# Moving the weight buffers of a two-stack transformer kernel by 64 bytes

## The reference, cut to what matters

```python
def first_block(x, ...):
    for layer in range(DEPTH):                  # 2 layers
        h = rms_norm(x, attn_norm[layer])
        if layer % 2 == 0:
            z = h @ w_in_e[i]                   # 1024 x 2072
            ...
            x = x + mix @ w_out_e[i]
        else:
            z = h @ w_qkv_o[j]                  # 1024 x 3072
            ...
            x = x + c_out.astype(x.dtype) @ w_out_o[j]
        h = rms_norm(x, ffn_norm[layer])
        gate, up = jnp.split(h @ w_gate_up[layer], 2, axis=-1)   # 1024 x 5632
        x = x + (jax.nn.silu(gate) * up) @ w_down[layer]         # 2816 x 1024
    return rms_norm(x, final_norm)

def compress_blocks(t, pe, w1, w2):
    ...
    return jax.nn.silu(blocks @ w1) @ w2        # w1: 2048 x 256
```

## Time and profile before

| what | value |
|---|---|
| median of 3 runs | 2921.04 us (2920.51 to 2929.26) |
| the profiled execution, device time | 2932.0 us |
| its span, first to last instruction | 2930.2 us |
| TensorE, matmuls | 2762.4 us busy (94%), 13516 matmuls |
| TensorE, weight loads | 2252.8 us busy (77%) |
| VectorE, ScalarE, GpSimd | 37%, 37%, 46% busy |
| mean granted TensorE clock | 0.967 |

### The profile page before, as it was taken

How to read it: one execution, slowest core, us unless ns; L and a number is a source line. 1 busy time by engine, 2 the same in 40 slices (tenths; PEclk the granted TensorE clock), 3 DMA queues, 4 the chain that set the end, 5 groups by cost and what they waited for, 6 DMA issues and landing times.

```text
span 2930.2 us, 37914 instructions
## 1 busy us (share of the span) xinstructions
PE 2762.4 (94%) x13516; PEld 2252.8 (77%) x13516; DVE 1078.1 (37%) x1941; ACT 1085.9 (37%) x1766; POOL 1345.6 (46%) x715
## 2 busy tenths in 40 slices
PE   7999999999999999999998999999978689999998
PEld 5756888888757888878767888888866588788886
DVE  5674322113563222023447234221074573432212
ACT  5665332223663322232243333332226343332221
POOL 4555444444384444444445544444433364344442
PEclk9999999999999999999889999999999799999998
DMA  4301323333202233323213312223312231223331
GB/s 156 122 2 39 97 95 100 100 108 97 86 1 83 93 100 100 101 79 102 71 37 101 108 58 86 92 95 105 104 51 79 80 125 62 65 94 100 100 101 64
DMA packets 69089, 251.77 MB, mean 86 GB/s; under 512 B 7672, under 2 KB 7928, under 8 KB 68736
## 3 DMA queue, kind: packets, MB, share of 16 engines
q1 hardware_dynamic: 67104, 244.35, 25.9%
q10 hardware_dynamic: 1888, 6.14, 0.6%
HBM read 248.36 MB, written 2.10 MB: 85 GB/s over the span
## 4 chain that ended last, share of the span: by engine, by line
PE 86%; DVE 9%; issue 2%; ACT 2%; POOL 1%; DMA 0%; DVEq 0%; POOLq 0%; ACTq 0%
PE ps L548 26%; PE ps L550 25%; PE ps L549 25%; PE ps L686 4%; PE ps L711 2%; PE ps L697 2%; DVE acc L1373 1%; DVE xl L1380 1%; POOL pr L514 1%; DVE u_r L1839 1%; DVE u_r L1837 1%; DVE tmpb L1862 0%; DVE pr L1473 0%; DVE y_mid L1683 0%; PE ps L656 0%
## 5 line engine op out<-in xcount | busy, mean ns | idle before, releaser
L467 POOL TENSOR_TENSOR w_lo<-w_raw,w_hi 128x1024 fp32r<-128x1024 f32 x462 | 1115.2, 2418 | 1382.5 <-ACT w_hi L980 1367.4
L548 PE MATMUL ps<-xh,w_hi 128*128 128x512 f32 x2384 | 940.0, 394 | 50.4 <-DVE xl L1380 21.6
L549 PE MATMUL ps<-xl,w_hi 128*128 128x512 f32 x2384 | 933.3, 391 | 0.0
L550 PE MATMUL ps<-xh,w_lo 128*128 128x512 f32 x2384 | 933.0, 391 | 0.0
L980 ACT ACTIVATE w_hi<-w_raw 128x1024 fp32r<-128x1024 f32 x462 | 484.5, 1053 | 531.0 <-PE ps L550 530.3
L548 PEld LDWEIGHTS ps<-xh,w_hi 128*128 128x128 f32 x2384 | 451.5, 189 | 150.3 <-issue 52.5
L549 PEld LDWEIGHTS ps<-xl,w_hi 128*128 128x128 f32 x2384 | 451.5, 189 | 94.3 <-issue 1.7
L550 PEld LDWEIGHTS ps<-xh,w_lo 128*128 128x128 f32 x2384 | 450.8, 189 | 94.9
L548 PE MATMUL ps<-hh,w_hi 128*128 128x512 f32 x704 | 273.9, 389 | 0.0
L550 PE MATMUL ps<-hh,w_lo 128*128 128x512 f32 x704 | 273.9, 389 | 0.0
L549 PE MATMUL ps<-hl,w_hi 128*128 128x512 f32 x704 | 273.9, 389 | 0.0
(11 more groups left out here) (258 smaller groups left out, 2910.4 us busy)
## 6 DMA issues: line engine op xcount, KB each, us to landing
w_raw<-weights_in SPq DMA_DIRECT2D x462, 512.0 KB, 3.4
x<-x_in ACTq DMA_DIRECT2D x4, 512.0 KB, 10.4
mem<-mem_in ACTq DMA_DIRECT2D x2, 1024.0 KB, 4.9
x_out<-x SPq DMA_DIRECT2D x4, 512.0 KB, 2.6
rope<-rope_in ACTq DMA_DIRECT2D x1, 512.0 KB, 11.8
tab<-tables_in ACTq DMA_DIRECT2D x2, 256.0 KB, 2.9
tab<-tables_in ACTq DMA_DIRECT2D x1, 384.0 KB, 12.4
small<-small_in ACTq DMA_DIRECT2D x1, 326.5 KB, 5.1
```

The source lines that it names most:

```text
L467: nc.gpsimd.tensor_tensor(w_lo[:, slot], w_raw[:, slot], w_hi.bitcast(f32)[:, slot], ALU.subtract).then_inc(lo_ready, 1)
L548: nc.tensor.matmul(dst, w_hi[:, slot, w], hi, start=first, stop=False)
L549: nc.tensor.matmul(dst, w_hi[:, slot, w], lo, start=False, stop=False)
L550: return nc.tensor.matmul(dst, w_lo[:, slot, w], hi, start=False, stop=last)
```

## The change

Two small buffers of 64 bytes per partition are allocated, one ahead of the three ring buffers and one behind them. Nothing reads or writes them. `w_raw`, `w_hi` and `w_lo` move up by 64 bytes and so begin on odd multiples of 64; everything allocated behind them moves up by 128 bytes and `x` stays. No instruction is added, removed or reordered, and no shape changes.

```diff
         x = sb("x", [P, KT, T])
+
+        sb("off_line", [P, 16])
         w_raw = sb("w_raw", [P, RING, CW])
         w_hi = sb("w_hi", [P, RING, CW], f32r)
         w_lo = sb("w_lo", [P, RING, CW], f32r)
+        sb("on_line", [P, 16])
         xl = sb("xl", [P, KT, T], f32r)
         rope = sb("rope", [P, 2, T])
         rstd = sb("rstd", [P, T])
```

## The result

The change makes the kernel slower: median 2941.2 us (2937.3 to 2943.5, 6 runs) against 2925.5 us (2920.5 to 2929.3, 6 runs, the three of the forecast and three more) before, a ratio of 1.0053, 95% interval 1.0038 to 1.0068. That is 15.7 us. The forecast was no change, 2921 us.

What follows compares the result with a forecast made beforehand. TensorE's matmuls, busy 2762.4 of 2930.2 us, were taken to bound the kernel. Every term was taken at 0, so the forecast stood on the median, 2921 us, with a range of 2905 to 2958.

Steps and rivals of the forecast that it cites:

- What bounds the kernel: TensorE's matmuls, busy 2762.4 of 2930.2 us; only their spacing, or a transfer or engine becoming late, could matter.
- Transfers: Weight chunks land 3.4 us after issue, with more than 10 us between issue and need; cost 0.
- ScalarE: `high` on the weight chunks takes 1.05 us and was expected not to depend on the address; cost 0.
- GpSimd: `low` on the weight chunks, cover thin only in the memory projections; taken at 0, at most 26 us.
- the price of a load by itself: Weight loads on TensorE beginning off a 128-byte line; price taken 0.
- Everything behind the weights: Buffers allocated after the weights move by 128 bytes, from an odd to an even multiple of 128; cost 0.
- the moving operands: They stay on multiples of 128 except 96 matmuls in `compress`; taken at 0, at most 9.6 us.
- The surcharge: 13.3 ns beyond the columns for each 512-column `product` matmul, 132 us over 9,936; change taken as 0.
- The argument from proportion: Time beyond the columns at full clock grows with stationary columns: 13.3 ns for 128, half for 64, whatever the moving columns.
- the block rival: Each weight load touches five 128-byte blocks instead of four, 3.3 ns each: 36 us slower, 2957 us; chance 0.11.
- The faster rival: Weight load and moving stream no longer collide in reading: up to 132 us less, 2789 us; chance 0.13.
- The 31-column loads: Half begin 124 bytes past a multiple of 128, yet all take 105 to 109 ns: no price for an off-line load.

Runs made afterwards that it cites:

- both off: Weights and every moving operand moved by 64 bytes (only the buffer ahead of the weights kept), against the kernel before: ratio 1.0001 (0.9992 to 1.0011).
- the first experiments: Three kernels against before, 64 bytes off: weights and moving operands 1.0001, only the moving operands 1.0053, only the raw chunks 1.0004.
- bare stream: Not the kernel: the reference's work left out, dense matmuls in the pattern of `product` with operand places varied; 226.7 ns at distance 0, 512 float32r columns.

## Why the prediction was wrong, point by point

**What bounds the kernel: right.** The time followed the spacing of the `product` matmuls, beside the granted clock of the attention stages, which varies from one execution to the next.

**Transfers, ScalarE, GpSimd, the price of a load by itself: right at 0.** The raw chunks alone off gave 1.0004, and both off 1.0001.

**Everything behind the weights, and the moving operands: not nothing.** The forecast took 128 bytes for a neutral step, since the moving operands stay on multiples of 128. The distance counts within 256 bytes: moving only what lies behind the weights by 128 costs 5.7 ns a matmul. In the change the weights move by 64 and the moving operands by 128, which makes the distance -64 and costs 2.2 ns; moving operands that had stayed modulo 256 would have made it 64, which costs 6.7. It is the second small buffer, placed to put them back on multiples of 128, that makes the distance: with the first alone both move by 64, and nothing is paid. In `compress`, where 64 stationary columns meet slices of the weights, the steps within a chunk went from 114.0 to 118.3 ns on average; that is 0.4 us for its 96 matmuls.

**The surcharge: named as the one place where the change could act, and priced wrongly.** The step that failed is the sentence that "whichever half the load begins in, the two meet for the same share of the time". It averages over two steady streams, and the spacing is not steady: it follows a repeating pattern, 226.7 each time at distance 0 and 226, 229, 232 in the change, and which pattern it is changes with the distance of the two starts. Whether the two wait for each other in it was not shown. The term was taken at 0 and measures 2.22 ns for each 512-column matmul: 9,936 x 2.22 = 22 us by the forecast's own count.

Of these 22 us the median shows 15.7 and the two profiled runs 11.3 (2943.3 - 2932.0). The traces tell where the rest went. Both have the same 13,516 matmuls in the same order and can be compared step by step. The 9,745 steps between 512-column matmuls of `product` that are at full clock in both are 21.3 us longer in sum, nearly the whole term. The steps outside `product` are 6.7 us shorter in sum, the rest of `product` about 3 us. A matmul at half clock pays nothing. And the attention stages, whose operands did not move against one another, ran at a better clock; here is one window after (row above: 69.7 us at 0.76 before), 1.2 us of it:

```profile
1447.00:1515.50 68.50, 63.14 (x385) 40.77 (x384) 29.41 (x106) 31.27 (x92) 35.29 (x32) 0.78 0.03 9
```

The same stage took 61.0 us at 0.89 in the profiled run with both off, so that it varies without any change of spacing. The clock also hides a part of the term in the medians: the runs of the change have a mean clock of 0.971 to 0.974, the 23 of before that ran beside the first experiments 0.965 to 0.971. At the same mean clock the term is whole. At 0.971 two runs of before took 2922.7 and 2924.0 us and one of the change 2943.5; at 0.970 six of before took 2924.4 to 2925.4 and three with the moving operands off, which have the distance of the change, 2947.0 to 2948.6. Why the kernels at distance -64 were granted the better clock stays open.

**The argument from proportion** (13.3 ns for 128 stationary columns, half for 64) held only where it was read. The bare stream has it again with 256 moving columns at distance 0 (120.0 and 113.3 ns), but at distance 64 the order is reversed (113.3 and 119.0), and with 512 moving columns 64 stationary ones cost more than 128 (230.0 and 226.7). It led to the block rival, whose sign was right and whose 3.3 ns per load was wrong, as was its mechanism: with both operands off, each load still touches one more block and nothing is paid. It is also why the rival stood at 36 us.

**The faster rival** rested on two reads that collide, which the runs fit but do not prove, and had the wrong sign: distance 0 was the best place of all that were tried at 512 columns, not the worst. Its argument against, that `compress` varies the distance without effect, held only for steps of whole 256 bytes, which do not count.

**The 31-column loads** were called a weak witness, and were: float32 shows the same spacing at all three distances tried.

**What the skill said.** By the Trainium skill (TensorE: Matmul & The Clock Gate, What happens when you issue a matmul) the load has a read port of its own and takes nothing from the stream, so that the place would be worth nothing. In bfloat16 and float32 no run contradicts it. In float32r the place is worth 2.2 to 6.7 ns in the whole kernel, and the measurement decides; that the 11 ns beyond 215.8 go with a repeated moving column does not tell whether the load has a part in them.

**The range and the chances.** 2941 lies within 2905 to 2958, but only because the range was stretched over the block rival, whose mechanism fell; that is luck. The chances gave "slower" 0.19, too little for a term for which, as the text said, no row showed another placement.

## What to carry to other kernels

In a stream of float32r matmuls with 512 moving columns that each load new weights, let the weights and the moving operands begin at the same place modulo 256 bytes, on multiples of 32; 128-byte alignment of each is not enough, and a stray buffer of 128 bytes between them costs 2% in this kernel. With 256 columns the bare stream was fastest at a distance of 64. After any change of allocations, compare the start-to-start distance of matmuls in a full-clock window before believing that "only addresses moved" is free. In bfloat16 and plain float32 none of this was seen.

## What the runs showed of the hardware that was not expected

At full clock a 512-column float32r matmul in such a stream costs 226.7 to 237.8 ns by the placement of its operands, and 215.8 ns when the moving operand is one column repeated. The cost of a placement depends on the number of moving columns: a distance of 64 bytes costs time with 512 columns (233.3 ns against 226.7), gains it with 256 (113.3 against 120.0), and has no effect with 384 (173.3). It is not paid load by load: moving one load of three back changed nothing (228.89 ns). Why the rhythm repeats as it does was not found.
